# A two-block transformer kernel on one core: the second output projection's left halves first, small products moved into the route, and another order of the steady expert loads

## The chip, the cores and the metric

The kernel runs on one core of a Trainium2 chip. The metric is the device time of one execution in microseconds; the kernel before has a median of 725.92 us over 3 runs (725.88 to 725.92).

## The reference

Two blocks in float32 on 256 tokens of width 1,024. The first has three mixers (pooling, sliding window, block attention), a gated merge and an output projection. The second has two attentions, a gated merge, its output projection, and a mixture of 16 experts with a router. Cut to what matters here:

```
merged = sigmoid(ga) * (o_fox @ w_branch_fox) + sigmoid(gb) * (o_sb @ w_branch_sb)
x = x + gate1 * (merged @ w_out)
h2 = rmsnorm(x, norm2_g) * (1.0 + scale2) + shift2
...
g_prob = softmax(h2 @ rg_w + rg_b)           # top 1 of 4 groups
e_logits = h2 @ re_w + re_b                  # top 2 of the group's 4 experts
for e in range(16):
    act = silu(h2 @ w_gate[e]) * (h2 @ w_up[e])
    out = out + combine[:, e:e + 1] * (act @ w_down[e])
x = rmsnorm(x + gate2 * out, final_g)
```

## The kernel before, in words

**Tiles.** Tokens lie in two tiles of 128 (t = 0, 1), and rows of 1,024 are worked in a left and a right half of 512 columns. Large products of the dense part are made of three matmuls in rounded float32 (L886 to L888): high by high, high by low, low by high. For this each weight chunk of 2,048 KB is split in four pieces: ACT writes the high part ("split", L1478) and DVE the low part ("split_low", L1822). A product waits for the pieces that it reads.

**One list of steps.** `plan` (from L91) writes STEPS by hand, and every engine goes through this one list and does its own share of each step, in that order. A "unit" is a group of PE matmuls into one PSUM bank; the engine that `evictor` names then takes the bank to SBUF. A unit may start when the unit that last had its bank is evicted: three units before, while banks 0 to 2 are used in turn, and four units before in the late part (`unit_bank_of`). Since each engine is in order, an eviction stands behind whatever the list puts before it on the same engine.

**The place of the change.** At the end of the dense part of the second block these units follow one another:
- `proj s t half`: the last branch product (12 matmuls of 512 columns), evicted by DVE with a gate and an addition (L1753, L1758).
- `mT 2 t half`: four transposes of merged; ACT writes the high part (L1376), DVE the low one (L1720).
- `wout 2 t half`: the output projection, 24 matmuls; DVE multiplies by a gate row and adds to x (L1767, L1768). The weight chunk of a half is `("wout", 2, half)`.
- `norm_half`, `norm`, `scale`: squares on ACT, root on ACT and DVE. `xn` scales x on ACT (L1497), `xn_lo` takes the low part on DVE (L1958), `zero` fills buffers of the expert loop on DVE (L1964).
- `xT t half`: transposes of x (L1026), the left ones evicted by ACT, the right ones by DVE. `rbias` (L1033): the router's bias. `logit` (L1043), `pick` (L1048): the router's products. `residual` (L1150): x copied to the four output banks.
- `route` on DVE picks group and experts (ready after L1987), `rank` (L1054 to L1058) counts the tokens before each, `slots` makes the one-hot matrix (L2016), and PE gathers the tokens with it (L1204).
- `ada c` (L992) and `mod c` (L979 for gate rows): products of the conditioning vector that `some_ada` strews over the list; `mod 10` makes a gate row that is wanted at the first expert's output.

**The experts.** Eight pairs of experts (0 to 7) run in a loop: gate and up of expert 0 and of expert 1 (L1241), the scatter of the pair before (L1184), and the two down matrices (L1289). Tokens sit in 64 slots for each expert. Six loads of 2,048 KB serve a pair: j = 0, 1 gate and up of its first expert, 2, 3 of its second, 4, 5 the downs; some places of odd pairs are made of several smaller buffers (gates, hT, mixed, con, attn, ada_acc, pw), each with a load of its own. All go through SP's one queue in order. A gate or up for pair n waits for the product of pair n - 2 that read its place (`gu_done`), a down for that of pair n - 1 (`down_done`). The order of issue is in `load_rest_of_round`: steps for pairs 0 and 1 written out, then a loop over pairs 2 to 5. Before the loop SP issues the loads of pairs 0 and 1 as places come free: j = 2 and 5 after `wout 2 1 0`, j = 3 and others after `wout 2 1 1`.

## Time and profile before

| | |
|---|---|
| median of 3 runs | 725.92 us |
| the profiled execution | 725.89 us |
| its span | 724.1 us |
| PE busy | 696.9 us (96%) |
| DVE, ACT busy | 397.3 us, 328.4 us |
| read from HBM | 200.59 MB |
| PE enters the expert loop at | 500.41 us |

The profiled execution takes 1.79 us more than its span. A row of the timeline has the start in us from the span's start, the duration, the engine, the line, the operation, and in brackets the engine's idle time before it with what ended it. A busy PE counts matmuls that overlap: twelve matmuls of 0.39 us follow one another at 0.23 us.

### The profile page before, as it was taken

The page shows a single profiled execution, that of the slowest core. Times are in us where ns is not written, and L with a number is a line of the kernel's source. Part 1 is how long each engine was busy: PE and PEld are TensorE (multiplying, and loading weights), DVE is VectorE, ACT ScalarE, POOL GpSimd, SP SyncE. Part 2 cuts the span into 40 slices and gives each one's busy share as a digit, 9 for nine tenths or more (in the row PEclk, how much of TensorE's full clock was granted, in tenths as well). Part 3 has the DMA queues.
Part 4 walks back from the last instruction along what each step waited for, and adds up shares of the span by engine and source line. Part 5 has one row for each costly group of instructions (what it writes and reads, how often), then busy time and mean ns, then how long its engine had stood idle before and what let it go on. Part 6 is the DMA issues. An engine that isn't in the chain of part 4 may idle for free.

```text
span 724.1 us, 10218 instructions
## 1 busy us (share of the span) xinstructions
PE 696.9 (96%) x4002; PEld 481.0 (66%) x4002; DVE 397.3 (55%) x722; ACT 328.4 (45%) x540; POOL 2.6 (0%) x5
## 2 busy tenths in 40 slices
PE   5999999999999999999999999998999999999894
PEld 3999989767777776799977776874344343343342
DVE  5654744776856978644665668656233323322325
ACT  6553434655758466344457776432123213213214
POOL 1000000000000000000000000000000000000000
PEclk9999999999999999999999999999999999999999
DMA  8974666753645549775344435769999999999961
GB/s 355 421 294 168 229 250 250 283 230 125 233 141 208 183 178 355 301 269 226 117 140 170 155 117 207 302 262 426 420 431 417 428 429 425 423 426 430 417 269 58
DMA packets 20011, 202.18 MB, mean 279 GB/s; under 512 B 2434, under 2 KB 3458, under 8 KB 7428
## 3 DMA queue, kind: packets, MB, share of 16 engines
q1 hardware_dynamic: 19248, 200.61, 69.5%
q10 hardware_dynamic: 724, 1.05, 0.4%
q8 instruction: 26, 0.43, 0.2%
q14 instruction: 13, 0.11, 0.0%
HBM read 200.59 MB, written 1.05 MB: 278 GB/s over the span
## 4 chain that ended last, share of the span: by engine, by line
PE 53%; DMA 3%; DVE 2%; ACT 2%; issue 1%; ACTq 0%; DVEq 0%
PE psum L1241 13%; PE psum L1289 7%; PE psum L886 7%; PE psum L887 7%; PE psum L888 7%; DMA ring<-in_expert_w_down 3%; PE psum L1204 3%; PE psum L1184 2%; PE psum L1125 1%; PE psum L992 1%; DVE ring_rounded L1822 1%; PE psum L1140 1%; PE psum L1266 0%; ACT ring_rounded L1478 0%; PE psum L1122 0%
## 5 line engine op out<-in xcount | busy, mean ns | idle before, releaser
L1822 DVE TENSOR_TENSOR ring_rounded<-ring,ring_rounded 128x1024 fp32r<-128x1024 f32 (+1 forms) x131 | 153.6, 1213 | 60.7 <-ACT ring_rounded L1478 60.7
L1478 ACT ACTIVATE ring_rounded<-ring 128x1024 fp32r<-128x1024 f32 (+1 forms) x132 | 129.6, 1038 | 8.9 <-PE psum L888 8.8
L886 PE MATMUL psum<-hT_rounded,ring_rounded 128*128 128x256 f32 x360 | 102.8, 286 | 0.0
L887 PE MATMUL psum<-work_rounded,ring_rounded 128*128 128x256 f32 x360 | 101.8, 283 | 0.0
L888 PE MATMUL psum<-hT_rounded,ring_rounded 128*128 128x256 f32 x360 | 101.8, 283 | 0.0
L887 PE MATMUL psum<-ring_rounded,hT_rounded 128*128 128x512 f32 (+1 forms) x224 | 86.5, 386 | 0.0
L1241 PE MATMUL psum<-ring,work 128*64 128x512 f32 x320 | 83.8, 592 | 1.2 <-issue 1.2
L886 PE MATMUL psum<-ring_rounded,hT_rounded 128*128 128x512 f32 (+1 forms) x208 | 83.2, 400 | 0.0
L888 PE MATMUL psum<-ring_rounded,work_rounded 128*128 128x512 f32 (+1 forms) x208 | 79.8, 384 | 0.0
L886 PEld LDWEIGHTS psum<-hT_rounded,ring_rounded 128*128 128x128 f32 x360 | 69.0, 192 | 3.0 <-issue 2.5
L887 PEld LDWEIGHTS psum<-work_rounded,ring_rounded 128*128 128x128 f32 x360 | 69.0, 192 | 0.1
L888 PEld LDWEIGHTS psum<-hT_rounded,ring_rounded 128*128 128x128 f32 x360 | 69.0, 192 | 0.0
L1241 PEld LDWEIGHTS psum<-ring,work 128*64 128x64 f32 x320 | 27.2, 137 | 55.4 <-issue 55.4
L1289 PE MATMUL psum<-ring,work 128*64 128x512 f32 x256 | 57.8, 597 | 3.4 <-DMA ring<-in_expert_w_down 3.2
L888 PE MATMUL psum<-ring_rounded,mixed_rounded 128*128 128x512 f32 x144 | 56.2, 390 | 0.0
L887 PEld LDWEIGHTS psum<-ring_rounded,hT_rounded 128*128 128x128 f32 x224 | 42.6, 190 | 7.3
L886 PEld LDWEIGHTS psum<-ring_rounded,hT_rounded 128*128 128x128 f32 x208 | 39.6, 191 | 11.7 <-issue 3.6
L888 PEld LDWEIGHTS psum<-ring_rounded,work_rounded 128*128 128x128 f32 x208 | 39.6, 190 | 8.2
L1289 PEld LDWEIGHTS psum<-ring,work 128*64 128x64 f32 x256 | 17.4, 136 | 35.3 <-issue 29.9
L2091 DVE SCALAR_TENSOR_TENSOR work<-attn,work,psum 64x512 f32<-64x512 f32 x8 | 6.0, 754 | 51.0 <-ACT attn L1554 51.0
L2103 DVE TENSOR_TENSOR work<-psum,gate_rows 64x512 f32<-64x512 f32 x16 | 10.9, 683 | 42.1 <-PE psum L1289 42.1
L886 PE MATMUL psum<-ring_rounded,work_rounded 128*128 128x512 f32 x80 | 32.0, 401 | 0.2 <-DVE ring_rounded L1822 0.2
(296 smaller groups left out, 1056.5 us busy)
## 6 DMA issues: line engine op xcount, KB each, us to landing
ring<-in_chunks SPq DMA_DIRECT2D x44, 2048.0 KB, 8.4
ring<-in_expert_w_down SPq DMA_DIRECT2D x16, 2048.0 KB, 16.7
ring<-in_expert_w_gate SPq DMA_DIRECT2D x12, 2048.0 KB, 16.4
ring<-in_expert_w_up SPq DMA_DIRECT2D x8, 2048.0 KB, 19.3
gates<-in_expert_w_up SPq DMA_DIRECT2D x8, 1024.0 KB, 22.2
hT<-in_expert_w_gate SPq DMA_DIRECT2D x4, 1024.0 KB, 16.9
mixed<-in_expert_w_gate SPq DMA_DIRECT2D x4, 1024.0 KB, 19.9
ring<-in_chunks SPq DMA_DIRECT2D x4, 512.0 KB, 7.5
```

Source lines behind the costliest of these rows:

```text
L886: nc.tensor.matmul(out, a[0], b[0], start=start, stop=False, skip_group_check=True)
L887: nc.tensor.matmul(out, a[0], b[1], start=False, stop=False, skip_group_check=True)
L888: return nc.tensor.matmul(out, a[1], b[0], start=False, stop=stop, skip_group_check=True)
L992: last = nc.tensor.matmul(b[32 * j:32 * j + 32, :], c_wide[:, at:at + 32], w[:, k, :], start=k < 4, stop=k >= 4, skip_group_check=True)
L1125: nc.tensor.matmul(b[:, 0:384], cs("suffix"), soft[:, h % 2, :], start=True, stop=False, skip_group_check=True)
L1184: return nc.tensor.matmul(out_bank[2 * t + half], as_rounded(slotT[odd][:, t * P:(t + 1) * P]), as_rounded(y[:, cols]), start=False, stop= ...
L1204: last = nc.tensor.matmul(b[:, k % 2 * T:(k % 2 + 1) * T], as_rounded(x[:, k * P:(k + 1) * P]), as_rounded(onehot[:, t].rearrange("p e s - ...
L1241: last = nc.tensor.matmul(gu_bank[e][HD * half:HD * half + HD, :], xg[:, k, (2 * odd + e) * SLOTS:(2 * odd + e + 1) * SLOTS], pair_rows(2 ...
L1289: last = nc.tensor.matmul(gu_bank[e][HD * half:HD * half + HD, :], actT[:, k, e * SLOTS:(e + 1) * SLOTS], pair_rows(4 + e, odd, k)[:, half ...
L1478: nc.scalar.activation(as_rounded(high_piece(c, q)), src[:, piece_of(c, q)], ACT.Copy).then_inc(chunk_hi, 1)
L1822: v.tensor_tensor(as_rounded(w[:, piece]), w[:, piece], was_rounded(high_piece(c, q)), ALU.subtract)\
L2103: left = v.tensor_tensor(y_pair[rows, 0:W512], gu_bank[e][0:HD, :], gate_rows[0:HD, 1, 0:W512], ALU.mult)
```

## The change

1. The second block's end is written out in a list of its own. All four projections `proj s` come with `mT 2 0 0` and `mT 2 0 1` among them and `ada 10` after; then the transposes of token tile 1; then `wout` in the order left of tile 0, left of tile 1, right of tile 0, right of tile 1. The splits of `("wout", 2, 1)` are placed by hand.
2. A `wout` unit waits for the first half of the transposes before its first matmul and for the second before its fifth group, not for both at once.
3. `rbias` goes behind the projection, `mod 10` between `residual 2` and `residual 3`; `zero` ahead of `scale 3 0` and `xn 3 0`; `xT 1 0` ahead of the last `wout`.
4. In the loop of loads, pairs 2 to 5, only load j = 0 goes ahead of the downs, and j = 1 behind them.

```diff
-PLACED = (FIRST, ROAMING, ("proj", "b"), ("vb",), ("qa",), ("wout", 1, 0), ("wout", 1, 1))
+PLACED = (FIRST, ROAMING, ("proj", "b"), ("vb",), ("qa",), ("wout", 1, 0), ("wout", 1, 1), ("wout", 2, 1))
...
     steps += [("sigmoid", 8), ("mods", 1)]
-    merge_and_out("s", 2)
-    steps += [("norm", 3, 0), ("scale", 3, 0)]
-    unit("rbias")
-    steps.append(("scale_router",))
+    unit("proj", "s", 0, 0)
+    unit("proj", "s", 0, 1)
+    unit("proj", "s", 1, 0)
+    unit("mT", 2, 0, 0)
+    unit("proj", "s", 1, 1)
+    unit("mT", 2, 0, 1)
+    some_ada()
+    unit("mT", 2, 1, 0)
+    unit("mT", 2, 1, 1)
+    split_placed(("wout", 2, 1), (0, 1), (0, 1))
+    unit("wout", 2, 0, 0)
+    split_placed(("wout", 2, 1), (2, 3), (2, 3))
+    steps.append(("norm_half", 3, 0))
     unit("wout", 2, 1, 0)
-    some_ada(mod_only=True)
+    unit("wout", 2, 0, 1)
+    steps += [("scale_router",), ("norm", 3, 0), ("norm_half", 3, 1), ("zero",), ("scale", 3, 0), ("xn", 3, 0)]
+    unit("xT", 1, 0)
+    unit("wout", 2, 1, 1)
     unit("xT", 0, 0)
     unit("xT", 0, 1)
-    steps += [("norm_half", 3, 1), ("xn", 3, 0), ("zero",), ("xn_lo", 0)]
-    unit("wout", 2, 1, 1)
-    steps.append(("norm", 3, 1))
-    unit("xT", 1, 0)
+    steps += [("norm", 3, 1), ("xn_lo", 0)]
+    unit("rbias")
+    unit("xT", 1, 1)
     unit("logit", 0)
-    steps.append(("residual", 0))
-    unit("xT", 1, 1)
+    steps += [("residual", 0), ("scale", 3, 1)]
     unit("pick", 0)
+    unit("logit", 1)
     steps.append(("residual", 1))
-    steps.append(("scale", 3, 1))
-    unit("logit", 1)
     unit("pick", 1)
-    steps += [("xn", 3, 1), ("residual", 2), ("route",), ("residual", 3), ("xn_lo", 1)]
+    steps += [("xn", 3, 1), ("residual", 2), ("route",)]
+    some_ada(mod_only=True)
+    steps += [("residual", 3), ("xn_lo", 1)]
...
-                        step(two_pairs * 2 + odd, odd, (gates_0, downs, gates_1))
+                        step(two_pairs * 2 + odd, odd, ((0,), downs, (1,), gates_1))
...
-                    pe.wait_ge(*evicted(("mT", blk, t, 1)))
                     for k in range(KD):
+                        if k % 4 == 0:
+                            pe.wait_ge(*evicted(("mT", blk, t, k // 4)))
```

The rest of the diff takes the second block out of `merge_and_out`, which keeps the first block's order.

SP, the body of the loop of loads for an even pair; the line of a load is L787 before and L791 with the change. Before:

```order
L787 ISA [waits gu_done]
L787 DMA ring<-in_expert_w_gate 128x4096
L787 DMA ring<-in_expert_w_up 128x4096 [waits gu_done]
L796 ISA
L787 ISA [waits down_done]
L787 DMA ring<-in_expert_w_down 128x4096
L787 ISA [waits down_done]
L787 DMA ring<-in_expert_w_down 128x4096
```

With the change:

```order
L791 ISA [waits gu_done]
L791 DMA ring<-in_expert_w_gate 128x4096
L800 ISA
L791 ISA [waits down_done]
L791 DMA ring<-in_expert_w_down 128x4096
L791 ISA [waits down_done]
L791 DMA ring<-in_expert_w_down 128x4096
L791 DMA ring<-in_expert_w_up 128x4096 [waits gu_done]
```

The up has gone from ahead of the two downs, and of their waits for PE, to behind them.

DVE, the end of the selection (L1987, L1992 with the change) up to the one-hot matrix (L2016, L2021). Before:

```order
L1987 TENSOR_TENSOR work<-work 128x32
L1958 SCALAR_TENSOR_TENSOR x_res_rounded<-x_res,stat,gates_rounded 128x1024
L1792 SCALAR_TENSOR_TENSOR work<-psum,work 128x2x16
L1794 TENSOR_SCALAR work<-work 128x2x16
L1795 TENSOR_SCALAR work<-work 128x2x4
L1796 TENSOR_REDUCE work<-psum 128x1
L2016 TENSOR_TENSOR work_rounded<-con,work 128x512
```

With the change:

```order
L1992 TENSOR_TENSOR work<-work 128x32
L1742 TENSOR_TENSOR gate_rows<-psum,gate_rows 128x512
L1963 SCALAR_TENSOR_TENSOR x_res_rounded<-x_res,stat,gates_rounded 128x1024
L1797 SCALAR_TENSOR_TENSOR work<-psum,work 128x2x16
L1799 TENSOR_SCALAR work<-work 128x2x16
L1800 TENSOR_SCALAR work<-work 128x2x4
L1801 TENSOR_REDUCE work<-psum 128x1
L2021 TENSOR_TENSOR work_rounded<-con,work 128x512
```

The eviction of `mod 10` into the gate rows (L1737 before) has come between the selection and the low part of the normalized rows.

PE, from the last transposes of x to the rank, with the change (the transposes are L1031, the bias L1038, the logits L1048, the residual copies L1155, the picks L1053, `mod 10` L983, the rank from L1059):

```order
L1031 MATMUL psum<-con,x_res 128x128 x8
L1038 MATMUL psum<-rt_w,mod 128x20 x8
L1031 MATMUL psum<-con,x_res 128x128 x4
L1048 MATMUL psum<-work 32x128 x8
L1155 MATMUL psum<-x_res,con 128x512
L1053 MATMUL psum<-pick,attn 128x20
L1048 MATMUL psum<-work 32x128 x8
L1155 MATMUL psum<-x_res,con 128x512
L1053 MATMUL psum<-pick,attn 128x20
L1155 MATMUL psum<-x_res,con 128x512
L983 MATMUL psum<-ada_acc,con 128x512
L1155 MATMUL psum<-x_res,con 128x512
```

The bias, which stood two products earlier, and `mod 10`, one product earlier, are now in this stretch.

## Rows read from the trace of the kernel before

**Rows 1.** The page: the DMA engines' busy share in 40 slices, in tenths.

```profile
DMA  8974666753645549775344435769999999999961
```

**Rows 2.** Windows: us, busy time (instructions) of each engine, PEclk, DMA share, GB/s.

```profile
470.00:480.00 10.00, 10.00 (x49) 8.09 (x49) 5.46 (x15) 3.47 (x8) 0.00 (x0) 1.00 0.32 98
...
640.00:660.00 20.00, 20.00 (x106) 10.02 (x104) 8.47 (x15) 7.06 (x10) 0.00 (x0) 1.00 1.01 431
```

**Rows 3.** The chain that ended last, in the expert loop: start, us, what.

```profile
552.59 13.73 PE psum L1241 x64
...
604.52 13.73 PE psum L1241 x64
...
690.82 7.02 PE psum L1241 x32
```

**Rows 4.** Timeline of PE, the down products of pair 6.

```profile
675.04 3.65 PE L1289 MATMUL psum<-ring,work 128*64 128x512 f32 x16 [1.94 <-DMA ring<-in_expert_w_down]
...
679.93 3.65 PE L1289 MATMUL psum<-ring,work 128*64 128x512 f32 x16 [1.24 <-DMA ring<-in_expert_w_down]
```

**Rows 5.** Timeline of SP: loads issued.

```profile
476.00 0.33 SPq L787 DMA_DIRECT2D ring<-in_expert_w_gate  x1
...
507.54 0.33 SPq L787 DMA_DIRECT2D ring<-in_expert_w_gate  x1
...
560.10 0.37 SPq L787 DMA_DIRECT2D ring<-in_expert_w_up  x1
...
573.12 3.77 SPq L787 DMA_DIRECT2D ring<-in_expert_w_down  x2
...
665.65 2.61 SPq L787 DMA_DIRECT2D pw<-in_expert_w_up  x1
```

**Rows 6.** Landing (last number) of loads issued at 476.00, 507.54, 560.10, 665.65; chunks 240-280.

```profile
ring<-in_expert_w_gate SPq DMA_DIRECT2D x1, 2048.0 KB, 8.0
...
ring<-in_expert_w_gate SPq DMA_DIRECT2D x1, 2048.0 KB, 9.7
...
ring<-in_expert_w_up SPq DMA_DIRECT2D x1, 2048.0 KB, 21.4
...
pw<-in_expert_w_up SPq DMA_DIRECT2D x1, 256.0 KB, 24.3
...
DMA to landing us min/median/max: 7.7/8.5/9.8
```

**Rows 7.** Timeline of PE, from the projection to the gather.

```profile
452.64 0.66 PE L1007 MATMUL psum<-con,gates 128*128 128x128 f32 x4 [0.82 <-DVE gates L1758]
...
463.00 0.50 PE L886 MATMUL psum<-ring_rounded,gates_rounded 128*128 128x512 f32 x1 [0.64 <-DVE x_res L1768]
...
468.57 1.86 PE L1033 MATMUL psum<-rt_w,mod 128*128 128x20 f32 x16
...
475.81 1.02 PE L979 MATMUL psum<-ada_acc,con 128*128 128x512 f32 x2
...
491.41 0.38 PE L1054 MATMUL psum<-work,con 128*128 128x32 f32 x2 [1.26 <-DVE work L1987]
...
494.00 1.22 PE L1204 MATMUL psum<-work_rounded,gates_rounded 128*128 128x256 f32 x8
```

**Rows 8.** Timelines of DVE and ACT in the same stretch.

```profile
457.42 2.35 DVE L1822 TENSOR_TENSOR ring_rounded<-ring,ring_rounded 128x1024 fp32r<-128x1024 f32 x2
...
477.35 0.68 DVE L1737 TENSOR_TENSOR gate_rows<-psum,gate_rows 128x512 f32<-128x512 f32 x1
...
478.41 1.14 ACT L1497 ACTIVATE gates_rounded<-x_res,stat 128x1024 fp32r<-128x1024 f32 x1
...
478.87 0.91 DVE L1964 MEMSET work<- 128x1024 f32 x1 [0.17 <-issue]
...
491.18 1.28 DVE L1958 SCALAR_TENSOR_TENSOR x_res_rounded<-x_res,stat,gates_rounded 128x1024 fp32r<-128x1024 f32 x1
...
493.09 0.69 DVE L2016 TENSOR_TENSOR work_rounded<-con,work 128x512 fp32r<-128x512 f32 x1
```

More of the change, by code:

```diff
@@ L211, in plan, with merge_and_out @@
     one, two, va, vb = ("wout", 1, 0), ("wout", 1, 1), ("va",), ("vb",)
-    def merge_and_out(br, blk):
-        first = blk == 1
-        if first:
-            split_placed(one, (0, 1))
-        unit("proj", br, 0, 0)
-        if first:
-            split_placed(one, (2,), (0,))
-        unit("proj", br, 0, 1)
-        if first:
-            split_placed(one, (3,), (1, 2))
-        unit("proj", br, 1, 0)
-        some_ada()
-        unit("mT", blk, 0, 0)
-        unit("mT", blk, 0, 1)
-        if first:
-            split_placed(one, (), (3,))
-            split_placed(va, (0, 1))
-        unit("proj", br, 1, 1)
-        if first:
-            split_placed(two, (0, 1, 2, 3), (0, 1, 2))
-        unit("wout", blk, 0, 0)
-        unit("mT", blk, 1, 0)
-        unit("mT", blk, 1, 1)
-        steps.append(("norm_half", 2 * blk - 1, 0))
-        if first:
-            split_placed(two, (), (3,))
-            split_placed(va, (2, 3), (0, 1))
-        unit("wout", blk, 0, 1)
+    def merge_and_out():
+        split_placed(one, (0, 1))
+        unit("proj", "a", 0, 0)
+        split_placed(one, (2,), (0,))
+        unit("proj", "a", 0, 1)
+        split_placed(one, (3,), (1, 2))
+        unit("proj", "a", 1, 0)
+        some_ada()
+        unit("mT", 1, 0, 0)
+        unit("mT", 1, 0, 1)
+        split_placed(one, (), (3,))
+        split_placed(va, (0, 1))
+        unit("proj", "a", 1, 1)
+        split_placed(two, (0, 1, 2, 3), (0, 1, 2))
+        unit("wout", 1, 0, 0)
+        unit("mT", 1, 1, 0)
+        unit("mT", 1, 1, 1)
+        steps.append(("norm_half", 1, 0))
+        split_placed(two, (), (3,))
+        split_placed(va, (2, 3), (0, 1))
+        unit("wout", 1, 0, 1)
     steps.append(("mods", 0))
-    merge_and_out("a", 1)
+    merge_and_out()
     steps += [("norm", 1, 0), ("norm", 2, 0)]
```

## The prediction

> **What bounds the kernel now.** I read the page first: the row of DMA shares is at 9 almost without a break from the last third on [rows 1]. So I took two stretches. From 640 to 660 us, in the expert loop, PE is busy all the time and so are the DMA engines (share 1.01, 431 GB/s); from 470 to 480 us, in the second output projection, the DMA engines are mostly idle (0.32, 98 GB/s) [rows 2]. At 431 GB/s a load of 2,048 KB (2.10 MB) takes 4.87 us; a pair of experts takes six, 29.2 us. Two pairs come back on PE after 51.93 us, from 552.59 to 604.52 us [rows 3], so a pair costs PE 26.0 us. The loads are the slower side, and PE lives on what was fetched ahead. The waits say where that lead ends: PE lost 3.2 us in two waits for a down matrix, both in pair 6 of 0 to 7, at 675.04 us (1.94) and 679.93 us (1.24) [rows 4]; no other wait for a load stands in the loop. After that the last pair's second gate and up start at 690.82 us [rows 3]; the last piece for them was issued at 665.65 us and landed 24.3 us later, at 689.95 us [rows 5, 6]. So the slack there is only 0.87 us. This is the number of this case: behind the stall that the change can remove stands the next transfer of the same saturated stream.
>
> **Part 1, the projection and the route.** In the new order PE does both left halves, then the right ones. The waits that this order could remove are 0.82 us before a transpose of merged, 0.64 us before the second product and 1.26 us before the rank [rows 7]; the router's bias (1.86 us from 468.57) and one modulation product (1.02 us from 475.81) leave the stretch between the products [rows 7]. The removal is not free, and I walked PE's, DVE's and ACT's lists in the new order with the old durations.
> First, DVE now has low halves of weights (2.35 us for two [rows 8]) ahead of the evictions of the transposes. Token 1's first transposes need an eviction of the projection behind one of them, which costs PE some 0.4 us, and its second ones need the bank of an earlier transpose, evicted behind another, some 1.3 us. That is 1.7 in place of 0.82 + 0.64 = 1.46.
> Second, the bias product takes the bank of a transpose of x that ACT evicts only after scaling x (1.14 us at 478.41), and that scaling waits for DVE's fill of zeros (0.91 us at 478.87, and two short operations), which now stands ahead of the root [rows 8]. I get a wait of 1.1 us.
> Third, the modulation product fills the wait before the rank, which is worth its 0.86 us on PE (475.81 to the next product at 476.67). Summed with the first two and with the order of the small products, the selection is ready some 0.6 us earlier.
> Fourth, DVE gives that back. The eviction of the modulation product (0.68 us at 477.35, 0.6 until the next can start) now stands between the selection and the low half of the last normalized rows (1.28 us at 491.18), and the rank's eviction and the one-hot matrix (0.69 us at 493.09, ready at 493.78) stand behind them [rows 8]. The one-hot matrix is thus ready when it was. Before, PE began its gather at 494.00 when the last ada product was through [rows 7]; now it would begin at about 493.8. **Gain at the loop's entry: 0.2 us.** Bounds: 3.1 if the two new waits (2.9 together) do not come, and a loss of 0.6 if the two are that much longer.
>
> **Part 2, the loads before the loop.** The left half's weights are free after two products, not three and the bias, so two expert loads start before 476.00 [rows 5] by a product (5.6 us, 463.00 to 468.57) and the bias [rows 7], and the idle DMA time there is used, at most 6.8 us (10 us at 0.32). But the first load inside the loop waits for pair 0's first gate and up, at 507.54 us, and landed at 517.24 [rows 5, 6]. A load into an empty queue takes 8.0 us (at 476.00), and the chunk loads between 240 and 280 us took 7.7 to 9.8, median 8.5 [rows 6]; I take 8.4. Issued at 507.3 this load lands at 515.7. So at most 1.5 us of the advance are left (517.24 - 515.7), and the rest is a hole of idle DMA. PE did not wait for loads here, so this alone changes no time.
>
> **Part 3, the order in the loop.** For pairs 2 to 5 the order was gate, up, two downs, then the second gate and up. Now only the first gate goes ahead of the downs. The downs move forward by one load, 4.87 us, which is more than the 1.94 us by which the first was late: the 3.2 us of waits go. The up moves back by two loads, 9.7 us, behind an issue that waits for PE's down product. The last pair's up takes the place of the last down of pair 6, 679.93 us; PE wants it one product (7.02 us [rows 3]) and a short transposition ahead of the second gate and up, which without the 3.2 us (below) is near 680.2, so it is just in time. The second gate and up of the last pair do not move in the stream. They still land at 689.95 us less whatever the whole stream has gained, and PE would want them at 690.82 - 3.2 - 0.2 = 687.4. **They are what is late next.**
> What has the stream gained? In loop pair 2 SP issues the gate and then stands until 573.12 us, when the first down product of that pair is through [rows 5]. The queue then holds only that gate. In the old order it landed one load before the up, which was issued at 560.10 and landed 21.4 later at 581.5, so at 576.6 [rows 5, 6]; less the 1.5 us of part 2 it is 575.1. The down behind it would land at 580.0 with the queue full; from an issue at 573.12 - 0.2 = 572.9 and 8.4 us it lands at 581.3. So a second hole of 1.3 us eats the advance: against 581.5 for the same place in the stream 0.2 us is left. From pair 3 on the backlog is longer (the stream slips 3 us on PE each pair) and I see no further hole.
>
> **The sum.** The last gate and up land at 689.95 - 0.2 = 689.75, and PE starts on them at 689.8 in place of 690.82. Everything behind is the same work: 1.0 us faster. The profiled execution took 725.89 us, 1.79 us around its span, and the median of the runs is 725.92, so both give **724.9 us**. As a formula: the gain is 0.83 us (the old slack less the start), plus 8.38 (581.5 - 573.12), plus the gain at entry, less the landing time from a nearly empty queue. Each us of the last two is a us of the end. With 7.7 and 9.8 us for the landing the gain is 1.7 or a loss of 0.4; with the bounds of part 1, 3.9 or 0.2.
> Against the landing times stands one rule. The Trainium skill, DMA: Bandwidth & Descriptors, Anatomy of one DMA, gives a fixed cost of about 2.0 us beside the bytes, for the GpSimd path. By that rule the landing would take 6.9 us and the estimate for the end would be 723.4 us. The trace disagrees: 8.0 less 4.87 is 3.1 us, on this queue.
>
> **The rivals.** About 0.2%, 1.45 us, is what a measurement of this kernel can tell from no change.
> - *The front end works.* The new waits on PE are my walk's, no row shows them. If they are 1 to 2.9 us shorter, PE enters that much earlier, issues the down of pair 2 earlier, and the second hole closes by as much: gains of 2.0 to 3.9 us, 722.0 to 723.9. For it: PE's own list is shorter between the products. Against it: DVE's list is longer where it matters. 0.2.
> - *The hole is short.* A landing of 7.7 us, the shortest of the rows: 1.7 us, 724.2. 0.1. The Trainium skill's rule above is the extreme of this case.
> - *Only the downs were late.* If the last gate and up land in time as well, PE bounds the loop: 3.2 + 0.2 = 3.4 us, 722.5. Against it stand 0.87 us of slack. 0.05.
> - *The queue runs dry, and it is slower.* One mechanism, in loop pair 2: SP waits behind the single gate, so the downs are issued into a queue that is about empty. At a landing of 9.4 us the gain is nil, and from 10.9 us the end is over 1.45 us later; 10.9 with 0.6 us lost at entry is 728.2. For it: loads of that size have taken up to 9.8 us [rows 6]. Against it: a median of 8.5, and that the 9.8 may hold some time behind another load. 0.12. The Trainium skill, same page, Rules for kernel authors, says to issue a load early and wait late so that the fixed cost overlaps; this order goes against it for the up matrices.
> - *It does nothing that reaches the end*: 725.9, within my forecast's band.
>
> **How the numbers follow.** My own case has 0.53, most of it between gains of 0.1 and 1.45 us, within 0.2%. Faster by over 0.2%: 0.2 + 0.1 + 0.05, 0.35. Slower by over 0.2%: 0.12. Within: 0.53. The range leaves out the tip of the fast cases and of the slow one: 722.8 to 726.5.
>
> **What would show it.** The page after should have no wait for a down, and instead a wait of some 2 us of the last pair's second gate and up product (L1246 in the new numbering) for a gate or up load, ending near 689.8. The issue of pair 2's down should stand at 572.9 with a landing of 8.4 us, and a DMA share below 1 just before 576 and between 507 and 511 us. PE should show waits near 455, 457 and 482 us and one of a few tenths before the gather. The forecast is wrong if PE enters the loop (500.41 before) earlier than 499.6 or later than 500.8, or if pair 2's down lands outside 580.9 to 581.9.

## The result, and the profile after

| | before | with the change |
|---|---|---|
| median, measured in turns (12 runs each) | 726.24 us (725.88 to 726.84) | 727.60 us (726.08 to 731.42) |
| ratio, 95% interval | | 1.0022 (1.0014 to 1.0030) |
| profiled execution | 725.89 us | 727.63 us |
| PE starts the last gate and up product | 690.82 us | 690.80 us |
| that product takes | 7.02 us | 8.78 us |

The change is slower by 1.4 us (0.2%) in the median, and its runs lie over 5.3 us where those of before lie within 1 us. Forecast were 724.9 us, and a range of 722.8 to 726.5. The last two rows hold the result in short: the last product starts when it did, and then TensorE is slower on it than before. Two runs in the slow state, one of "front fix" (787 us) and one of "pair 2 in the old order" (1,784 us), are in none of the medians and ranges below; with them these two medians would be 725.74 and 725.47 us.

The page of the changed kernel: the busy times, the granted clock and the DMA engines' share in 40 slices.

```profile
span 725.8 us, 10222 instructions
...
PE 698.9 (96%) x4002; PEld 482.0 (66%) x4002; DVE 397.5 (55%) x722; ACT 328.2 (45%) x540; POOL 2.6 (0%) x5
...
PEclk9999999999999999999999999999999999999998
DMA  8974666753645549765344335898999999999951
```

The same matmuls are 2.0 us busier than before (696.9), though nothing was added to them. The DMA row of the page reads 8, 9, 8 in slices 26 to 28 (454 to 508 us), where before [rows 1] it reads 7, 6, 9: the loads before the loop come earlier, and a hole follows.

Waits of PE from 500 to 700 us, summed by line: total, times, longest.

```profile
PE psum L1246 <- DMA pw<-in_expert_w_up: 2.6, 1, 2.6
PE psum L1246 <- issue: 1.3, 1, 1.3
```

The two waits for a down [rows 4] are gone. In their place stands one of 2.6 us for the last piece of the last up matrix: "what is late next".

Timeline of PE, first the front (the answers to [rows 7]), then the loop's first product and the last gate and up.

```profile
455.51 0.66 PE L1011 MATMUL psum<-con,gates 128*128 128x128 f32 x4 [0.20 <-DVE gates L1763]
457.25 0.66 PE L1011 MATMUL psum<-con,gates 128*128 128x128 f32 x4 [1.08 <-DVE mixed_rounded L1725]
...
482.13 1.96 PE L1038 MATMUL psum<-rt_w,mod 128*128 128x20 f32 x16 [1.08 <-ACT work L1412]
...
491.18 0.38 PE L1059 MATMUL psum<-work,con 128*128 128x32 f32 x2 [0.41 <-DVE work L1992]
...
494.25 1.19 PE L1209 MATMUL psum<-work_rounded,gates_rounded 128*128 128x256 f32 x8 [0.41 <-issue]
...
500.71 3.65 PE L1246 MATMUL psum<-ring,work 128*64 128x512 f32 x16 [1.33 <-issue]
...
690.80 1.07 PE L1246 MATMUL psum<-hT,work 128*64 128x512 f32 x1 [2.58 <-DMA pw<-in_expert_w_up]
```

All five waits in the front that the prediction named are there. The last row is a single matmul of 1.07 us; its fellows in the product before it took 0.59 us.

Times of two executions can be compared only after their common part is laid level. A row of work that is the same in all these kernels, some 20 us ahead of the first wait above, is that of the last small product of the attention, before and with the change:

```profile
435.06 0.39 PE L1143 MATMUL psum<-attn,gates 128*64 128x128 f32 x4
```

```profile
435.49 0.39 PE L1148 MATMUL psum<-attn,gates 128*64 128x128 f32 x4
```

So the profiled execution of the changed kernel was already 0.43 us late before anything of the change began; over the profiled executions of all versions this row lies between 434.72 and 435.87 us. Below it is called the common row. Counted from it, PE enters the expert loop at 65.22 us with the change and at 65.35 before: 0.13 us earlier, where the times from the span's start (500.71 and 500.41) say 0.3 later. The last gate and up product starts 0.45 us earlier (255.31 for 255.76).

SP's loads and their landings (last number), as [rows 5, 6]: the first ahead of the loop, the first inside it, pair 2's down, and the last piece.

```profile
468.86 0.33 SPq L791 DMA_DIRECT2D ring<-in_expert_w_gate  x1
...
507.83 0.33 SPq L791 DMA_DIRECT2D ring<-in_expert_w_gate  x1
...
573.44 3.77 SPq L791 DMA_DIRECT2D ring<-in_expert_w_down  x2
...
669.78 3.49 SPq L791 DMA_DIRECT2D pw<-in_expert_w_up  x1
```

```profile
ring<-in_expert_w_gate SPq DMA_DIRECT2D x1, 2048.0 KB, 8.3
...
ring<-in_expert_w_down SPq DMA_DIRECT2D x1, 2048.0 KB, 8.9
...
pw<-in_expert_w_up SPq DMA_DIRECT2D x1, 256.0 KB, 21.0
```

The first loads start 7.1 us earlier than before (468.86 for 476.00), but the first one in the loop lands at 516.1 us, 1.1 us earlier than before (517.24); counted from the common row, 7.6 and 1.5 us. Pair 2's down, the second of these landings, comes into a nearly empty queue and is in at 582.3: the one load ahead of it, the gate issued at 559.96, lands 15.8 us later, at 575.8.

Windows around these holes and behind the wait: us, busy time (instructions) of PE, PEld, DVE, ACT, POOL, then PEclk, DMA share, GB/s.

```profile
500.00:507.90 7.90, 7.19 (x34) 2.58 (x36) 3.85 (x7) 0.63 (x2) 0.00 (x0) 1.00 0.63 258
...
575.00:577.00 2.00, 2.00 (x12) 0.65 (x10) 0.27 (x1) 0.00 (x0) 0.00 (x0) 1.00 0.69 270
...
688.00:690.80 2.80, 0.22 (x3) 0.00 (x1) 0.75 (x1) 0.48 (x1) 0.00 (x0) 1.00 1.07 444
690.80:694.00 3.20, 3.20 (x8) 0.97 (x10) 0.00 (x0) 0.00 (x0) 0.00 (x0) 0.51 1.03 440
694.00:697.00 3.00, 3.00 (x16) 1.04 (x14) 0.00 (x0) 0.00 (x0) 0.00 (x0) 0.95 1.00 426
```

The first two rows are the two holes (DMA share 0.63 and 0.69). The last three are what the prediction did not have. While PE waits for the last up, its clock still reads 1.00; when it starts, the granted clock is 0.51, the lower of its two levels (1.2 of 2.4 GHz), for 3.2 us, and is back at 0.95 in the next three. The matmuls of this product run in pairs, and its second pair starts 0.86 us after the first (691.66 for 690.80), where in the product before the pairs follow at 0.43 us. The chain of waits puts the sum in one row:

```profile
690.80 8.78 PE psum L1246 x32
```

8.78 us in place of 7.02 [rows 3]: 1.76 us, which is also the 1.74 us between the two profiled executions (727.63 less 725.89), since their products start at the same time.

So the theory to be tested had two parts. **A: the sum of the prediction is right as a formula** (the end moves with the moment when pair 2's down is issued and with its landing), and this execution simply filled it with 573.44 and 8.9. **B: the rest is TensorE's clock**, which falls behind a wait in some executions and not in others. The rival to B is that the scatter comes from the transfers, and that the low clock is only seen beside it.

### The profile page after: what moved, and what is told of

It reads as the page before. It is cut to its first block, busy times and chain, and to the rows that moved or that the text cites. A ratio compares the mean times of both kernels' runs of the same rounds, so it can differ in the third digit from the quotient of the medians.

```text
span 725.8 us, 10222 instructions
## 1 busy us (share of the span) xinstructions
PE 698.9 (96%) x4002; PEld 482.0 (66%) x4002; DVE 397.5 (55%) x722; ACT 328.2 (45%) x540; POOL 2.6 (0%) x5
## 4 chain that ended last, share of the span: by engine, by line
PE 51%; DMA 3%; DVE 2%; ACT 2%; SPq 2%; issue 1%; ACTq 0%; DVEq 0%
PE psum L1246 13%; PE psum L890 7%; PE psum L1294 7%; PE psum L891 7%; PE psum L892 7%; PE psum L1209 3%; DMA pw<-in_expert_w_up 3%; PE psum L1189 2%; SPq L791 2%; PE psum L1130 1%; PE psum L996 1%; PE psum L1145 1%; DVE ring_rounded L1827 0%; PE psum L1271 0%; ACT ring_rounded L1483 0%
```

## The experiments

All were timed in turns with the kernel before, whose median was 726.23 us for the first four, 726.37 for the next four and 726.35 for the last four. "Loop entered" and "start", when PE starts the last gate and up product, are read in the one profiled execution, by the chain of waits; "from the common row" is the loop's entry less that execution's common row. Each of these groups of four ran on another chip; the medians of before differ by 0.14 us between them.

| kernel | us, median (range) | ratio, 95% interval | loop entered | from the common row | start | wait before it |
|---|---|---|---|---|---|---|
| the change | 727.60 (726.08 to 731.42) | 1.0022 (1.0014 to 1.0030) | 500.71 | 65.22 | 690.80 | 2.58 |
| front only | 725.79 (724.56 to 728.33) | 0.9993 (0.9984 to 1.0001) | 501.96 | 66.74 | 691.26 | none |
| loop only | 727.46 (725.01 to 728.48) | 1.0012 (1.0003 to 1.0021) | 500.52 | 65.37 | 690.47 | 2.60 |
| pair 2 in the old order | 725.40 (723.85 to 727.81) | 0.9990 (0.9977 to 1.0002) | 500.35 | 65.16 | 688.74 | 1.32 |
| a wait per piece | 723.59 (723.02 to 726.16) | 0.9968 (0.9956 to 0.9980) | 500.48 | 65.21 | 687.89 | 0.35 |
| front fix | 725.71 (723.73 to 727.37) | 0.9991 (0.9981 to 1.0001) | 499.67 | 63.82 | 689.16 | 2.42 |
| front fix, a wait per piece | 721.79 (720.96 to 721.94) | 0.9939 (0.9926 to 0.9952) | 498.55 | 63.83 | 685.86 | 0.2 |
| front fix, six fillers | 726.67 (726.52 to 727.37) | 1.0007 (0.9998 to 1.0016) | 499.12 | 63.87 | 691.58 | none |
| loop only, a wait per piece | 722.71 (722.67 to 723.22) | 0.9953 (0.9940 to 0.9966) | 500.65 | 65.38 | 687.75 | none |
| front fix, three fillers | 724.84 (724.13 to 725.29) | 0.9980 (0.9971 to 0.9989) | 498.85 | 63.89 | 689.03 | 0.34 |
| per piece, front fix, pair 2 old | 721.32 (720.89 to 721.94) | 0.9929 (0.9916 to 0.9943) | 499.73 | 63.86 | 686.88 | none |
| the same, splits placed | 719.50 (719.24 to 719.88) | 0.9908 (0.9893 to 0.9923) | 497.19 | 62.32 | 684.31 | none |
| front fix, pair 2 old | 722.58 (722.22 to 722.94) | 0.9948 (0.9935 to 0.9962) | 499.39 | 63.80 | 687.83 | 1.30 |

**1. The front alone.** The change, with the loop of loads as before:

```diff
-                        step(two_pairs * 2 + odd, odd, ((0,), downs, (1,), gates_1))
+                        step(two_pairs * 2 + odd, odd, (gates_0, downs, gates_1))
```

> The changed kernel with the old order of the steady loads (gate, up, two downs, second gate and up). Theory: the new front costs nothing and the loop's new order is what hurts. With the old order there is no hole at pair 2, the stream keeps the 1.1 us by which its first load in the loop landed earlier, and pair 6 waits for its downs less (some 1.7 us in place of 3.2): about 1.1 us faster than before, 724.8. Rival (the front is at fault, since PE entered the loop at 500.71 in place of 500.41): 0.3 us or more slower than before, 726.5.

Measured 725.79 us, 0.4 us from the kernel before: neither the gain expected nor the rival's loss. Its profiled execution shows one source of the scatter of its runs over 3.8 us. Timeline of PE (the bias product and the rank), and windows between the two rows (columns as above):

```profile
481.85 1.96 PE L1038 MATMUL psum<-rt_w,mod 128*128 128x20 f32 x16 [1.06 <-ACT work L1412]
...
492.46 0.38 PE L1059 MATMUL psum<-work,con 128*128 128x32 f32 x2 [0.40 <-DVE work L1992]
```

```profile
484.00:486.00 2.00, 2.00 (x21) 0.98 (x20) 1.52 (x6) 0.00 (x0) 0.00 (x0) 0.65 1.04 434
486.00:488.00 2.00, 2.00 (x20) 1.22 (x18) 0.55 (x4) 1.15 (x1) 0.00 (x0) 0.50 0.99 418
```

Behind the new wait at the bias product, 1.06 us, the granted clock is 0.65 and then 0.50. From the bias product to the rank PE takes 10.61 us; in the change's profile, where the same wait of 1.08 us brought no fall, it takes 9.05 (482.13 to 491.18). That is 1.6 us, and counted from the common row the loop is entered 1.5 us later (66.74 for 65.22). So the clock can fall in this front too, and the end is not the only place. With the old order of the loads most of it was made good on the way: the last product starts only 0.3 us later than before (256.04 for 255.76 from the common row), since the waits for the downs, which take up lateness of PE, are 2.1 us in place of 3.2. Why the median missed the 724.8 us is not settled by this one execution.

**2. The loop alone.** The kernel before, with the reverse of that line.

> The kernel before with the new order of the steady loads alone. Theory: pair 2's first down is issued at 573.1 into a nearly empty queue and lands 8.9 us later, at 582.0; the stream is then 0.6 us later than before, the last gate and up land near 690.6, PE waits 2.9 us for them, the clock is halved for a few us behind that wait (1.8 us): 727.4 to 727.8. Rival (the front is at fault): faster than before, 723 to 725.

Measured 727.46 us: as expected, and within 0.14 us of the whole change. The loop's order by itself makes the slowdown. Its profiled execution took 725.57 us, 1.9 below its own median. Timeline of PE and a window:

```profile
690.47 0.64 PE L1241 MATMUL psum<-hT,work 128*64 128x512 f32 x1 [2.60 <-DMA pw<-in_expert_w_up]
```

```profile
690.80:694.00 3.20, 3.20 (x18) 1.05 (x16) 0.00 (x0) 0.00 (x0) 0.00 (x0) 1.00 1.00 425
```

The wait is the same and ends on the same load, but the clock stays at 1.00, and 18 matmuls lie in or reach into this window where the change's execution has 8. The product takes 7.09 us there. Behind one wait of 2.6 us the clock fell in one execution and not in the other.

**3. The second hole.** The change, with pair 2 in the old order (the loop of loads written out for that):

```diff
+                for pair in range(2, 6):
+                    step(pair, pair % 2, (gates_0, downs, gates_1) if pair == 2 else ((0,), downs, (1,), gates_1))
```

> The changed kernel with the old order of loads for pair 2 alone (pairs 2 to 5 written out, 3 to 5 in the new order). Theory: no hole at pair 2, the stream stays 1.1 us ahead, the last gate and up land near 688.9, PE waits about 1 us for them, too short for the clock to fall: 1.9 us faster than before, 724.0 to 724.3. Rival (the clock falls behind any wait at that place): 725.8. Rival (the hole is elsewhere): as the changed kernel, 727.6.

The hole is gone (pair 2's down now lands 12.3 us behind its issue, in a full queue), and the last product starts at 688.74, 2.1 us earlier than with the change (1.8 from the common row). Its runs stand in three groups: five at 723.85 to 724.20 us, three at 725.40 to 725.54 and three at 727.63 to 727.81, with a mean granted clock of 0.997, 0.995 and 0.993. The first group is what was expected; the steps of 1.5 and 2.2 us come with the clock. The expected number came true in fewer than half of the runs, and the median, 725.40, missed it.

**4. A wait per piece.** In odd pairs the gate and the up lie in up to five smaller buffers, and PE waited for all of them before the first matmul. Here each piece has its own semaphore, and PE waits for it before the first matmul that reads it:

```diff
+                        if odd:
+                            part_loaded(pe, 2 * e, before, k)
+                            part_loaded(pe, 2 * e + 1, before, k)
```

> The changed kernel, with a semaphore for each piece of an odd pair's gate and up, and PE waiting for a piece only before the first matmul that reads it. Theory: the last gate and up product starts at 687.8 on the pieces that landed at 683 to 687 and reaches the last piece (landed at 690.75) after it is there: no wait, no fall of the clock, 3.0 + 1.8 us less than the changed kernel: 722.9, which is 3.3 us faster than before. Rival (the end is set by something other than the wait for the last piece): within 1 us of the changed kernel.

723.59 us, 0.7 more than expected, and the start at 687.89 us: all of the 2.58 us but 0.35 was a wait for bytes that were not needed yet. The last piece landed at 691.6 us in this execution, 3.7 us after the product had begun. Between the two profiled executions lie 4.6 us (727.63 less 723.02): 2.9 are the earlier start (690.80 less 687.89), and 1.7 are the clock, for the product takes 7.09 us. The medians lie 4.0 us apart. The bias wait is still in this kernel, and so are signs of a fall: four of its six runs have a mean clock of 0.992 to 0.994, one of them at 726.16 us.

**5. The front fix.** The bias product takes a bank that ACT evicts behind the scaling of x. With the transposes placed ahead of that scaling, ACT evicts them first:

```diff
-    steps += [("scale_router",), ("norm", 3, 0), ("norm_half", 3, 1), ("zero",), ("scale", 3, 0), ("xn", 3, 0)]
+    steps += [("scale_router",), ("norm", 3, 0), ("norm_half", 3, 1)]
     unit("xT", 1, 0)
+    steps += [("zero",), ("scale", 3, 0), ("xn", 3, 0)]
```

> The changed kernel, with the unit that transposes x of tile 1 placed ahead of the fill of zeros, the root and the scaling in the list, so that ACT evicts it before it scales x. Theory: the 1.08 us wait of the bias product goes, PE enters the loop 1.06 us earlier (499.65), pair 2's down is issued that much earlier into the same nearly empty queue, so the last gate and up land 1.06 us earlier and the end comes 1.06 us earlier: 726.5. The runs scatter less upwards, since the clock no longer falls behind that wait. Rival (the entry does not matter since the end is bound by the saturated stream): 727.6, as the changed kernel.

The 1.08 us wait is gone (the bias product follows the transposes at once, at 481.25 us), and the loop is entered at 499.67 us. That is 1.04 us earlier, but 1.40 counted from the common row (63.82 for 65.22), and all six profiled executions with this repair agree with it (63.80 to 63.89). 725.71 us is 1.9 us better than the change, more than the 1.1 expected: the last product starts 2.0 us earlier from the common row, 1.4 by the entry and the rest by a landing of pair 2's down in 8.2 us where the change's took 8.9. Timeline of PE:

```profile
689.16 0.64 PE L1247 MATMUL psum<-hT,work 128*64 128x512 f32 x1 [2.42 <-DMA pw<-in_expert_w_up]
```

The wait at the end is nearly as long as ever, and its runs still scatter, from 723.73 to 727.37 us.

**6. Front fix and a wait per piece.**

> The same, with PE waiting for the pieces of an odd pair's gate and up one by one. Theory: PE is the bound from entry to end, so the 1.06 us of the entry come off the 723.6 of the kernel with pieces: 722.5, 3.7 us faster than before. Rival (another transfer is next): 723.5.

721.79 us, 0.7 better than expected; the repair had been counted as 1.06 us and is worth 1.4. With both waits gone the scatter is gone too: 1.0 us over all five runs.

**7. More work in place of the wait, six.** This tests B directly: PE does six transposes of the identity ahead of the second gate and up of each odd pair, so that it works where it waited.

```diff
+                if odd:
+                    for _ in range(6):
+                        nc.tensor.matmul(gu_bank[1][:, 0:P], ident, ident, start=True, stop=True, skip_group_check=True)
```

> The kernel of the front repair (whole waits, no pieces) with work added: six transposes of the identity (128x128, about 0.11 us each, 0.65 us together, their result is overwritten) ahead of the second gate and up product of each odd pair. Theory: the stream is held up by pair 1's fillers alone, 0.65 us, while PE's wait in the last pair shrinks from 2.6 to some 0.6 us and the clock stays up, so that more work takes less time: 0.65 - 1.8 = 1.1 us less than the front repair, 725.4. Rival (the clock has no part in it): 0.65 us more than the front repair, 727.2.

726.67 us, a miss: I had priced the six at about half of what they took. A transpose leaves two records of some 0.11 us, and the expected 0.11 us is one of them. Timeline of PE, the last of the four times:

```profile
690.08 1.50 PE L1263 MATMUL psum<-con 128*128 128x128 f32 x12
```

By the chain of waits, which takes off what overlaps, it is four times 1.34 us, 5.4 in all. That is more than the wait, so that PE became the bound and the end moved with it. Still the scatter is gone: 0.85 us over 11 runs, against 3.6 with the front fix alone. Since nothing waits for a load any more, this alone does not tell the clock from the transfers. Inconclusive on the time, it called for the half dose.

**8. The loop's new order with a wait per piece, the front as before.**

> The kernel before with the new order of the steady loads and the waits for pieces, its own front kept. Theory: no wait for a load of more than 0.5 us is left, the 3.2 us of before are saved, and PE bounds the loop: 723.0, 0.5 us more than with the repaired front (its entry is 0.8 us later and has no risk at the bias product). Rival (the new front is what made the version with pieces fast): 725 or more.

722.71 us, as expected. It is better than number 4, which has the new front as well, by 0.9 us: once hardly anything in the loop waits, the new front is worth less than the old one, though PE enters the loop 0.17 us earlier with it. I put that down to its bias wait and the clock behind it (four of the six runs of number 4 have a mean clock below 0.995, none of the five here); number 6, the new front without that wait, is 0.9 us better than number 8.

**9. More work in place of the wait, three.** As 7, with `range(3)`.

> Front fix with three identity transposes (about 0.67 us in all, by half of what six cost, 1.34) ahead of the second gate/up of each odd pair. Theory (TensorE's clock falls behind a wait of over about 2 us, in some executions and not in others): the last pair's second gate/up arrives up to 0.7 us later than the 689.2 us of the front fix, TensorE's own wait falls from 2.4 to about 1 us or less, the granted clock stays at 1.0 or falls in few executions, and the median is 724.6 to 725.2, below the 725.74 of the front fix although the kernel does more. Rival (the clock has no part, the spread comes from the transfers): the work is simply added, up to 0.7 us, so that the median is 725.7 to 726.4 and the spread of the front fix (4 us) stays.

724.84 us, within what B gives and outside what the rival gives: **the kernel does more than the front fix alone (4026 matmul instructions for 4002 on the page, two for each of the 12 transposes) and takes 0.9 us less in the median.** In 87 of the 121 pairs of a run of each the one with fillers is the faster. Timeline of PE:

```profile
687.85 0.83 PE L1263 MATMUL psum<-con 128*128 128x128 f32 x6
689.03 0.64 PE L1247 MATMUL psum<-hT,work 128*64 128x512 f32 x1 [0.34 <-DMA pw<-in_expert_w_up]
```

The wait is 0.34 for 2.42 us, and the product still starts when its load lands. Counted from the common row that is 0.76 us later than in number 5 (254.07 for 253.31), as expected from pair 1's fillers (0.67 us), which hold up the stream. So an execution without a fall should be slower with the fillers, and it is: its fastest run took 724.13 us, that of number 5 723.73. What went are the long times: 725.29 is its highest, where number 5 has 727.37. The order of the transfers is the same and PE waits for the same load, so late transfers would show in both; they leave room for the 1.2 us over which these runs lie, not for the 3.6 of number 5. So the rival to B falls. The "over about 2 us" of the theory is not a measured limit: in number 1 the clock fell behind 1.06 us, and no run here finds one.

**10. A wait per piece, the front fix and pair 2 in the old order.**

> A wait per piece, the front fix and the loop's order of before for pair 2. Theory: with a wait per piece the loop is bound by TensorE from end to end, so pair 2's order hardly matters: 721.5 to 721.8 us, as the 721.79 without it. Rival: the queue still sets the time through its advance, and the 1.3 us that the old order of pair 2 gave with whole waits comes again: 720.5.

721.32 us, between the two and nearer to the theory; all five runs (720.89 to 721.94) lie above the rival's 720.5. From the common row the last product starts 0.13 us earlier than in number 6. Once PE waits piece by piece, pair 2's order hardly counts.

**11. The same, with the second projection's splits placed by hand,** so that DVE's low halves stand where they delay no eviction (ACT's high halves are placed too, all four ahead of the first product):

```diff
+    left = ("wout", 2, 0)
+    split_placed(left, (0, 1, 2, 3))
     unit("proj", "s", 0, 0)
+    split_placed(left, (), (0,))
     unit("proj", "s", 0, 1)
+    split_placed(left, (), (1,))
     unit("proj", "s", 1, 0)
...
+    split_placed(left, (), (2,))
     some_ada()
     unit("mT", 2, 1, 0)
     unit("mT", 2, 1, 1)
+    split_placed(left, (), (3,))
```

> As the one before, with the second output projection's splits placed by hand so that the transposes of the merged rows of tile 1 no longer wait (0.20 and 1.08 us in the change's profile). Theory (each microsecond of TensorE's waits in the front comes off the time once the loop is bound by TensorE): the loop begins 1.3 to 1.7 us earlier and the time is 720.0 to 720.5 us. Rival: the last load's arrival is still what ends the time, the queue starts at the same moment, and the gain in the front turns into a wait for a load: 721.3 to 721.8.

719.50 us, 1.8 less than number 10 and 0.9% less than the kernel before. It is 0.5 us better than the range expected. Timeline of PE:

```profile
454.64 1.09 PE L1024 MATMUL psum<-con,gates 128*128 128x128 f32 x8
...
497.19 7.09 PE L1262 MATMUL psum<-ring,work 128*64 128x512 f32 x32 [1.35 <-issue]
```

The eight transposes of tile 1 follow one another without the 0.20 and 1.08 us, and the loop is entered at 497.19, which is 1.5 us earlier than in number 10 from the common row (62.32 for 63.86). Its four runs lie within 0.64 us. This is the fastest version and the one to keep.

**12. The front fix and pair 2 in the old order, waits for whole loads.**

> Front fix and pair 2 in the order of before, waits for whole loads. Theory: the last pair's second gate/up arrives about 1.3 us earlier than with the front fix alone (about 687.9), TensorE waits about 1 us for it, too short for the clock to fall in most executions: median 722.5 to 723.5. Rival: the clock falls behind any wait near 1 us too, and then the median stays at 725 us or over.

722.58 us, 722.22 to 722.94. Timeline of PE:

```profile
687.83 0.64 PE L1246 MATMUL psum<-hT,work 128*64 128x512 f32 x1 [1.30 <-DMA pw<-in_expert_w_up]
```

Against number 3 it lacks only the bias wait; the wait at the end is the same (1.30, 1.32). Number 3 ran in three groups over 4 us, this one within 0.7. So in number 3 the falls came with the wait in the front, and a wait of 1.3 us at the end, behind full-size products, brought none in these five runs.

## Why the prediction was wrong, step by step

**What bounds the kernel, and what is late next: right.** The downs' waits went, the last gate and up took their place with 2.58 us (forecast "some 2 us"). They land at 690.75 us (issued at 669.78, 21.0 us to landing), 0.8 later than before, where 0.2 earlier was forecast; 0.43 of that is how late this execution was at the common row, the rest is part 3. Numbers 4, 6, 8, 10 and 11 show the other side: with little or no wait in the loop it takes 187.1 to 187.4 us from entry to the last product, in all five, and the 190.41 us of before (690.82 less 500.41) are that and its 3.2 us of waits.

**Part 1, the front: right, its sum too.** Forecast were 0.4 and 1.3 us at the transposes of merged (0.20 and 1.08 measured), 1.1 at the bias (1.08), a rank wait that shrinks (1.26 to 0.41) and a few tenths at the gather (0.41). The sum shows only when the executions are laid level at the common row. Then the selection is ready 0.66 us earlier (forecast 0.6; DVE's last row of it starts at 490.84, against 491.07), the one-hot matrix is level (0.06 earlier; 493.46 against 493.09), and PE enters the loop 0.13 us earlier (forecast 0.2). Three executions with this front and no fall in it entered 65.16, 65.21 and 65.22 us behind the common row, three with the front of before 65.35, 65.37 and 65.38. Two steps of its working do not hold as written. The gain of 0.6 us at the selection can't be added up from the terms shown: 1.46 less 1.7, less 1.1 and plus 0.86 is a loss of 0.5, so that 1.1 us rest on "the order of the small products" alone. And the two new waits are 2.8 us together, not 2.9, while the loss of 0.6 given as a bound does not follow from waits that much longer (0.2 less 2.9 would be a loss of 2.7). So the 0.6 us at the selection came true, but what is written does not derive it.

**Part 2: right.** Forecast 515.7, measured 516.1 us for the first load in the loop, 0.43 of it the late common row. The 7.6 us of advance shrink to 1.5, as forecast.

**Part 3, the second hole: right in mechanism, its landing 0.5 us too short.** Forecast was a down issued at 572.9 that lands 8.4 us later, at 581.3; it was issued at 573.44, took 8.9 and landed at 582.3. By the prediction's own test this was out of bounds (580.9 to 581.9). By its own formula the gain was then 0.83 + 8.38 - 0.32 - 8.9 = 0.0, with the issue 0.32 us later than before's 573.12 (0.11 earlier from the common row). The last product started at 690.80 for 690.82. The formula holds in all four executions that have the hole and a wait for whole loads at the end, with nothing fitted. Ready = 690.82 - (0.83 + 8.38 + 573.12 - issue - landing):

| | issue | landing | formula | measured |
|---|---|---|---|---|
| the change | 573.44 | 8.9 | 690.83 | 690.80 |
| loop only | 573.25 | 8.8 | 690.54 | 690.47 |
| front fix | 572.38 | 8.2 | 689.07 | 689.16 |
| front fix, three fillers | 572.27 | 8.3 | 689.06 | 689.03 |

Four more executions have the hole but do not wait for the last piece (numbers 4, 6, 7 and 8). There pair 2's down took 10.0, 9.9, 8.4 and 8.4 us, and the last piece landed where the formula puts it, within 0.1 us. So the forecast 8.4 was a fair middle of eight landings between 8.2 and 10.0, and an execution can fall 1.6 us behind it: a loss of 0.6 us, at the edge of the forecast's range.

These landings, less 4.87 for the bytes, leave 3.3 to 5.1 us, part of it time behind the gate that was still under way. The Trainium skill, DMA: Bandwidth & Descriptors, Anatomy of one DMA, gives about 2.0 us for another path; here, on SP's queue, no run comes near it. The rival that rested on it (723.4 us) is out.

**The sum: the step that failed is its sentence "Everything behind is the same work".** It is the same work at another clock. The prediction traded two waits of 1.94 and 1.24 us, with a product of 16 matmuls between them, for one of 2.58 us, and priced waiting PE at its length alone. Behind the long one the granted clock was 0.51, and the last product took 8.78 us for 7.02. In the profiled execution the forecast was missed by 2.7 us: 0.4 is the late common row, 0.6 is lost gain (0.5 by the landing, 0.1 at the entry), and the rest is this 1.76. Counted from the common row the change is 1.76 - 0.45 = 1.3 us slower, which is the 1.4 us between the medians. No term of the sum had the 1.76, nor any rival. "The queue runs dry" (chance 0.12) names a mechanism that is there, but in this execution its price was 0.5 us; it does not make the change slower. Without the fall the formula gives 725.9 us, and the fastest of the 12 runs, 726.08, with the highest mean clock, 0.997, is there; the two lowest clocks of the 12, 0.989 and 0.993, go with the four slowest, 728.45 to 731.42.

**What is shown and what is argued.** That the new waits cause the scatter is shown: it goes when the wait at the end is filled with work (numbers 7 and 9) or split (6, 8, 10, 11), when the bias wait is removed beside a short one at the end (12 against 3), and it comes with the loop's order alone (2). That it is by the clock rests on the rows of the change beside those of number 2, and on number 9 against 5, the one pair in which PE goes on waiting for the load; in the others a spread of the landings, up to 1.8 us at pair 2's down, would be hidden as well. Some of the change's own scatter can be that. What a fall costs is read from rows at either level in two places: 1.7 us at the end (8.78 against 7.09 behind a wait as long) and 1.6 in the front. Where the clock fell in the other runs, of which only a mean clock is known, is argued. As an estimate from these rows, 3.2 us at half the clock is 0.002 of a mean over 725.8 us, the step from 0.997 to 0.995. What decides in which execution it falls was not settled: behind waits of 1.06 and 1.08 us, and of 2.58, 2.60 and 2.42, it fell in one of each and not in the others. The Trainium skill, TensorE: Matmul & The Clock Gate, Part 1, says of a kernel's start that the number of matmuls at the lower clock varies from run to run of the same kernel. No run here shows such a count twice for one kernel; what varies here is the mean clock of the change's runs (0.989 to 0.997) and their time, by 5.3 us. A wait per piece with the loop's old order was not tried, and how the fall goes with the length of the wait was not measured either.

## What to carry to other kernels

Price a wait of TensorE by its length and by the clock behind it: here one wait of 2.58 us cost more than two of 1.94 and 1.24 with matmuls between them, and the cost shows in the scatter and the median, often not in the one profiled execution. Before two profiles are compared by their times, lay them level at a row ahead of the change: here 0.43 us of another origin turned a gain of 0.13 at the loop's entry into a loss of 0.3. When a kernel's runs spread wider after a change, look at the mean clock of each run before looking for a cause in the transfers. When a load is late, ask first whether the consumer needs all of it: here a wait for each piece, at the matmul that reads it, was worth 3.9 to 4.8 us (numbers 4, 6 and 8), more than any order of the loads; and an engine that evicts in order should have the eviction that someone waits for ahead of the long operation that nobody waits for.

## What the runs showed of the hardware that was not expected

- TensorE at half its clock behind a wait: 0.51 for 3.2 us behind 2.58 us of waiting, and 0.65 and 0.50 in two windows of 2 us in which PE was busy all the time, behind a bias product that had waited 1.06.
- 24 matmul instructions more, put where PE had waited, took 0.9 us off the median (725.71 to 724.84) and 2.1 us off the slowest run.
- A mean clock below the highest is no proof of lost time by itself: the kernel before had a run at 0.993 and 726.68 us beside one at 0.998 and 726.23.
- A load of 2,048 KB into a nearly empty queue took 8.2 to 10.0 us in eight executions at the same place of the program, and where PE waited for whole loads each tenth of it was a tenth of the last product's start.
- Executions of the same work differ by up to 1.15 us at 435 us into it (434.72 to 435.87), while the 65 us from there to the loop's entry repeat within 0.1 us for one front where the clock did not fall.
